# Two feed-forward pairs, a lambda and a last passage: three small reorderings in a two-layer streaming encoder step

## The chip, the cores and the metric

The kernel runs on one core of a Trainium2 chip. The metric is the device time of one execution in microseconds (us), lower is better. Five engines work side by side: TensorE (PE in the rows; PEld is its weight load), VectorE (DVE), ScalarE (ACT), GpSimd (POOL) and SyncE (SP), each with an in-order queue. They meet through semaphores only.

## The reference

Two layers run on 512 prompt frames and 32 sample frames, which lie side by side as 544 columns. Layer 0 mixes with gated linear attention, layer 1 with differential attention (two softmaxes of each head, subtracted with a learned lambda). Each mixer is followed by a gated feed-forward with a causal convolution of width 3:

```python
h = modulate(rms_norm(x, norm_mix[i]), sh1, sc1)
if i % N_MIXERS == 0:
    mix, S_fin = gla_mixer(h, S0, ...)
else:
    q, k, v = diff_project(h, diff_w_in[j], diff_q_norm[j], diff_k_norm[j])
    lam = jnp.exp(jnp.sum(lq1 * lk1)) - jnp.exp(jnp.sum(lq2 * lk2)) + lam_init
    o = diff_attend(q, k, v, 0, lam)          # softmax 0 - lam * softmax 1
    o = rms_norm(o, diff_norm[j]) * (1.0 - lam_init)
    mix = einsum('bthe,hed->btd', o, diff_w_out)
x = x + gt1[:, None, :] * mix
h = modulate(rms_norm(x, norm_ffn[i]), sh2, sc2)
f, cst_new = conv_ffn(h, cst, ffn_w_in[i], ffn_conv_w[i], ffn_conv_b[i], ffn_w_out[i])
x = x + gt2[:, None, :] * f
```

All data are float32. Projections are made as three matmuls of split operands (high with high, low with high, high with low part).

## The kernel before

**Blocks and units.** All projections form one stream of weight blocks of 256 columns (`BL`), each with an own load by SyncE into `w_raw` (three buffers), a `split` on ScalarE (the high part, into `w_hi` or `w_third`) and a `low` on VectorE (the low part, into `w_lo`). TensorE waits for `low` of a block before the block's first unit. A block has four units: two column tiles `t` of 128 by two halves of the 544 columns (272 each). A unit is 24 matmuls of 128x272 (eight contraction tiles by three) into one of the eight banks of the PSUM. `place_units` gives each unit its bank; `U_PREV` is the unit that had the bank before, and `bank_free` makes TensorE wait until it is evacuated.

**Pairs.** The first two blocks after each norm are run as a pair of eight units, in `first_pair`: all first halves (units 0 to 3), then all second halves (units 4 to 7), since the norm finishes the columns half by half. Units 0, 1, 4, 5 belong to the pair's first block, 2, 3, 6, 7 to its second. Units 0, 1 and 4, 5 follow the norm's tiles as these are made. `PAIR_BANKS` gives their banks. In between stands `stats`: the sums of squares of half 0 and 1 go to banks 4 and 5, where ScalarE's `half_root` reads them.

**The norm at such a place.** For each half and each of eight tiles: VectorE scales (`half_scaled`, `sq`), ScalarE adds the shift (`half_modulated`, `h_hi`), VectorE makes the rest (`h_lo`). `half_tiles(which, half, ks)` issues this on VectorE. A norm needs the squares of all eight tiles of `xT` (ScalarE's `square`), which GpSimd adds up in `acc`, before TensorE can sum them over partitions.

**The feed-forward** (`ffn`). The up blocks alternate between the u and gate halves. For each tile ScalarE copies the unit of the first half into `up` (`head_in`), then the second half's pieces, and makes the first convolution term; VectorE adds the other two. For gate tiles ScalarE also makes the SiLU and casts the product (`act_hi`), each of which waits for VectorE. After the norm ScalarE first makes the SiLU of `c_row`. The evacuation order of the pair is units 0, 1, 4, 5, then 2, 6, 3, 7. The third up block, `("up", l, 0, 2)`, had banks 4, 5, 7, 6 of its own, all later up blocks have banks 0 to 3 in turn.

**The lambda.** Ahead of layer 1's attention VectorE makes the two sums of the lambda (`lam_ok`), ScalarE the exponentials (`lam_exp`), VectorE the rest (`lam_done`). ScalarE waits for this and then evacuates the pair of the first keys and queries, `("dk", 0)` and `("dq", 0)`, squares first and then the scaled values into `kT` and `qT`.

**The last passage.** The output projection of the attention ends with `doutB`: 16 units in four banks in turn, eight for half 0 and eight for half 1, which VectorE adds to `xT` (`last_out`). The norm of half 0 begins while the units of half 1 are still being added; the order of both on VectorE and of squares, shifts and the two half splits on ScalarE is written out by hand.

Of the kernel before, what the change touches and what calls it, by code (L numbers as in the profile page):

```python
# [10 lines left out]
ALU = mybir.AluOpType  # L11
# [9 lines left out]
KT = D // P  # L21
TP, TS = 512, 32
T = TP + TS
# [17 lines left out]
SCALE = HD ** -0.5  # L41
LAM_INIT = 0.8 - 0.6 * math.exp(-0.3)
# [51 lines left out]
BL = stream_blocks()  # L94
BN = {name: n for n, name in enumerate(BL)}
# [9 lines left out]
PAIRS = [(("gout", 2), ("gout", 3)), (("down", 0, 3, 2), ("down", 0, 3, 3)), (("dk", 0), ("dq", 0))]  # L105
PAIRS += [(("up", l, 0, 0), ("up", l, 0, 1)) for l in range(DEPTH)]
PAIR_OF = {a: b for a, b in PAIRS}
PAIRED = [x for pair in PAIRS for x in pair]
PAIR_BANKS = [0, 1, 2, 3, 7, 6, 0, 1]
block_kt = lambda n: CH[BL[n][2]] if BL[n][0] == "down" else KA if BL[n][0] == "doutA" else KT  # L110

UNITS = []
# [10 lines left out]
FIRST_U, LAST_U = [min(us) for us in BU], [max(us) for us in BU]  # L123
# [6 lines left out]
def place_units():  # L130
    bank, prev = [], []
    last, counts, small = {}, {True: 0, False: 0}, 0
    for u, (n, t, half) in enumerate(UNITS):
        kind = BL[n][0]
        if BL[n] in PAIRED:
            at = u - FIRST_U[BN[next(a for a, z in PAIRS if BL[n] in (a, z))]]
            b = at % 4 if kind in ("gout", "down") else PAIR_BANKS[at]
        elif kind == "up" and BL[n][2:] == (0, 2):
            b = (4, 5, 7, 6)[u - FIRST_U[n]]
        elif BL[n] in KMAJOR:  # L140
            b = u - FIRST_U[n]
        elif kind in ("qk", "v", "r", "dq", "dk", "dv", "doutA"):
            b = small % 2
            small += 1
        else:
            b = (u - FIRST_U[n]) % 4
        bank.append(b)
        prev.append(last.get(b))
        last[b] = u
    evac_no = [0] * len(UNITS)  # L150
    for n, name in enumerate(BL):
        if name[0] == "up" and name in PAIRED:
            us = BU[n] if name not in PAIR_OF else [BU[n][i] for i in (0, 2, 1, 3)]
        elif name in PAIR_OF:
            us = range(FIRST_U[n], FIRST_U[n] + 8)
        elif name in PAIRED:
            us = []
        else:
            us = range(FIRST_U[n], LAST_U[n] + 1)
        for u in us:  # L160
            on_act = BL[UNITS[u][0]][0] in ACT_KINDS
            counts[on_act] += 1
            evac_no[u] = counts[on_act]
    return bank, prev, evac_no
# [44 lines left out]
H_BASE = (0, KT, 2 * KT, 4 * KT, 6 * KT)  # L209
# [17 lines left out]
block_units = lambda name: BU[BN[name]]  # L227
pair_units = lambda name: list(range(FIRST_U[BN[name]], FIRST_U[BN[name]] + 8))
# [61 lines left out]
def hybrid_stream_step(nc, A, O):  # L290
    ctx = ExitStack()
    with ctx:
# [3 lines left out]
        def sem(name):  # L296
            return ctx.enter_context(nc.semaphore(name))
# [4 lines left out]
        h_hi = sb("h_hi", [P, KT, T], F32R)  # L302
        h_lo = sb("h_lo", [P, KT, T], F32R)
# [61 lines left out]
        up = sb("up", [P, 2, W + 2], c=f)  # L365
# [9 lines left out]
        st = sb("st", [P, 96], c=d)  # L375
# [91 lines left out]
        up_ok, conv_ok, silu_ok, prod_ok, act_hi_ok, act_ok = (sem(x) for x in (  # L467
            "up_ok", "conv_ok", "silu_ok", "prod_ok", "act_hi_ok", "act_ok"))

        lam_ok, lam_exp, lam_done = sem("lam_ok"), sem("lam_exp"), sem("lam_done")  # L470
        hsum_ok, hlog_ok, hinv_ok, heads_ok = (sem(x) for x in ("hsum_ok", "hlog_ok", "hinv_ok", "heads_ok"))
        sc_ok, mx_ok, p_ok, a_ok, a_turned, a_out, av_ok, av_out = (sem(x) for x in (
            "sc_ok", "mx_ok", "p_ok", "a_ok", "a_turned", "a_out", "av_ok", "av_out"))
# [686 lines left out]
        def _(act):  # L1160
# [48 lines left out]
            def half_modulated(which, half, ks):  # L1209
                l, sub = which // 2, which % 2  # L1210
                for k in ks:
                    act.wait_ge(xs_ok, XS_BASE[which] + KT * half + k + 1)
                    for grp, c in ((0, slice(0, HALF)),) if half == 0 else ((0, slice(HALF, TP)), (1, slice(TP, T))):
                        ins = A_(h_hi[:, k, c], sq[:, k % 2, c], ACT.Identity, bias=ada[:, l, 3 * sub * KT + k, grp:grp + 1])
                    ins.then_inc(h_hi_ok, 1)
# [48 lines left out]
            def evacuate_all(us):  # L1264
                for u in us:
                    evacuate(u)
# [301 lines left out]
            def heads_turned(p, part_, bank):  # L1568
# [4 lines left out]
                else:  # L1573
                    A_(hi[:, k:k + 2, TP:T], ps[:, bank, 0:2 * TS].rearrange("p (j t) -> p j t", j=2), ACT.Identity,
                       scale=st[:, 1:2]).then_inc(od_hi_ok, 1)

            act.wait_ge(lam_ok, 1)
            A_(st[:, 4:6], st[:, 2:4], ACT.Exp).then_inc(lam_exp, 1)
            act.wait_ge(lam_done, 1)
            us, dv0 = pair_units(("dk", 0)), block_units(("dv", 0))  # L1580
            evacuate_all(us[0:7])
            head_norms(0, 0)
            evacuate(us[7])
            head_norms(0, 1)
# [46 lines left out]
            half_modulated(3, 0, (1,))  # L1631
            square(3, 4, 1)
            square(3, 5, 1)
            half_modulated(3, 0, (2,))
            square(3, 6, 1)
            square(3, 7, 1)
            half_modulated(3, 0, (3,))
            split(BN[("up", 1, 0, 1)], 0)
            half_modulated(3, 0, (4, 5))
            split(BN[("up", 1, 0, 1)], 1)  # L1640
# [7 lines left out]
        def _(dve):  # L1648
# [86 lines left out]
            def half_tiles(which, half, ks):  # L1735
                l, sub = which // 2, which % 2
                for k in ks:
                    if k == 0:
                        dve.wait_ge(rstd_ok, sums_at(which, half))
                        half_scaled(which, half, 0)  # L1740
                    if k + 1 < KT:
                        half_scaled(which, half, k + 1)
                    dve.wait_ge(h_hi_ok, NORM_H[which] + KT * half + k + 1)
                    for grp, c in ((0, slice(0, HALF)),) if half == 0 else ((0, slice(HALF, TP)), (1, slice(TP, T))):
                        ins = STT(out=h_lo[:, k, c], in0=sq[:, k % 2, c], scalar=ada[:, l, 3 * sub * KT + k, grp:grp + 1], in1=f32(h_hi[:, k, c]),  # L1745
                                  op0=ALU.add, op1=ALU.subtract)
                    ins.then_inc(h_ok, 1)
# [61 lines left out]
            def evacuate_all(us):  # L1809
                for u in us:  # L1810
                    evacuate(u)
# [263 lines left out]
            dve.wait_ge(nc_stored, 16)  # L2075
            dve.wait_ge(lam_loaded, 16)
            dve.wait_ge(h_ok, H_BASE[4])
            TT(h_smp2[:, :, :], f32(h_hi[:, :, TP:T]), f32(h_lo[:, :, TP:T]), ALU.add).then_inc(smp_ok, 1)
            lp = lam_in[:, :, :].rearrange("p (a b) d -> p a b d", b=2)
            step.then(TT(lp[:, :, 0, :], lp[:, :, 0, :], lp[:, :, 1, :], ALU.mult))  # L2080
            dve.tensor_reduce(st[:, 2:4], lp[:, :, 0, :], AX_X, ALU.add).then_inc(lam_ok, 1)
            dve.tensor_scalar(st[:, 0:1], q_gain, SCALE, None, ALU.mult)
            dve.tensor_scalar(st[:, 1:2], d_gain, 1.0 - LAM_INIT, None, ALU.mult)
            dve.wait_ge(lam_exp, 1)
            step.then(TT(st[:, 6:7], st[:, 5:6], st[:, 4:5], ALU.subtract))
            step.then(dve.tensor_scalar(st[:, 7:8], st[:, 6:7], -LAM_INIT, None, ALU.add))
            STT(out=st[:, 8:9], in0=cpart("isc1"), scalar=st[:, 7:8], in1=cpart("isc0"), op0=ALU.mult, op1=ALU.add).then_inc(lam_done, 1)

            def heads_normalised(p, idx):
                if p >= NPAIR:  # L2090
# [140 lines left out]
            last_out(DOUT_B[KT:KT + 4])  # L2231
            half_tiles(3, 0, (0,))
            last_out(DOUT_B[KT + 4:KT + 6])
            half_tiles(3, 0, (1,))
            last_out(DOUT_B[KT + 6:])
            half_tiles(3, 0, range(2, KT))
            low(BN[("up", 1, 0, 1)])
            half_tiles(3, 1, range(KT))
            ffn(1)
# [121 lines left out]
```

## Time and profile before

| what | us |
|---|---|
| median of 3 runs | 1397.14 (1396.92 to 1397.16) |
| span of the profiled execution | 1395.4 |
| runs' median less this span | 1.74 |
| TensorE busy | 1374.3 |
| VectorE busy | 950.7 |
| ScalarE busy | 655.0 |
| GpSimd busy | 89.5 |

The span runs from the first to the last instruction of one profiled execution; the runs' time holds what lies around it as well. The TensorE clock was granted in full all the way (1.000). An idle time of an engine other than TensorE costs nothing unless TensorE ends up waiting for it.

### The profile page before, as it was taken

What the parts mean: (1) busy time and instruction counts of PE and PEld (TensorE: products, weight loads), DVE (VectorE), ACT (ScalarE), POOL (GpSimd) and SP (SyncE); (2) the same over time, 40 slices, a digit from 0 to 9 for tenths busy, and PEclk for the clock granted to TensorE, in tenths of its full rate; (3) what the DMA queues carried; (4) which work ended last, traced back from release to release, by engine and by line L of the source; (5) the groups of instructions that cost most, each with busy time, mean ns of one, the idle gap of its engine ahead of it and who ended that gap; (6) DMA issues with size and microseconds to landing.
All of it is one profiled execution on the core that took longest, in us unless ns stands there. A gap on an engine that the chain in (4) does not pass through costs nothing.

```text
span 1395.4 us, 26322 instructions
## 1 busy us (share of the span) xinstructions
PE 1374.3 (98%) x10882; PEld 1294.7 (93%) x10882; DVE 950.7 (68%) x1595; ACT 655.0 (47%) x1458; POOL 89.5 (6%) x149
## 2 busy tenths in 40 slices
PE   8999999999999999999999999999899999999999
PEld 6878888999999999999888888889899999999999
DVE  5688677479988788678765646576798654554554
ACT  5543434366553353351565555653665542552430
POOL 0000000210000000000300000000300000000000
PEclk9999999999999999999999999999999999999999
DMA  9644542244445444534523224112244222223222
GB/s 378 238 167 147 178 152 84 72 171 135 161 144 171 171 157 133 193 115 148 182 107 106 103 98 137 63 62 93 96 161 135 77 78 91 91 69 114 76 71 103
DMA packets 38014, 182.42 MB, mean 131 GB/s; under 512 B 4294, under 2 KB 6854, under 8 KB 26632
## 3 DMA queue, kind: packets, MB, share of 16 engines
q1 hardware_dynamic: 22984, 126.98, 26.4%
q0 software_dynamic: 14912, 53.78, 11.1%
q8 instruction: 86, 1.41, 0.4%
q14 instruction: 32, 0.26, 0.1%
HBM read 172.82 MB, written 7.91 MB: 130 GB/s over the span
## 4 chain that ended last, share of the span: by engine, by line
PE 91%; DVE 4%; ACT 3%; issue 1%; DMA 0%; POOL 0%; SPq 0%; DVEq 0%; POOLq 0%; ACTq 0%
PE ps L656 27%; PE ps L658 26%; PE ps L657 26%; PE ps L1065 2%; PE ps L1115 1%; DVE sq L1732 1%; DVE h_lo L1745 1%; PE ps L1024 1%; PE ps L1087 1%; PE ps L913 1%; PE ps L909 1%; ACT w_hi L1173 1%; PE ps L694 1%; PE ps L900 1%; PE ps L746 1%
## 5 line engine op out<-in xcount | busy, mean ns | idle before, releaser
L658 PE MATMUL ps<-h_hi,w_lo 128*128 128x272 f32 x2048 | 592.5, 289 | 0.0
L656 PE MATMUL ps<-h_hi,w_hi 128*128 128x272 f32 x1952 | 569.1, 292 | 5.5 <-ACT up L1452 1.7
L657 PE MATMUL ps<-h_lo,w_hi 128*128 128x272 f32 x1952 | 561.3, 288 | 0.0
L658 PEld LDWEIGHTS ps<-h_hi,w_lo 128*128 128x128 f32 x2048 | 385.0, 188 | 0.0
L656 PEld LDWEIGHTS ps<-h_hi,w_hi 128*128 128x128 f32 x1952 | 367.4, 188 | 15.8 <-issue 6.7
L657 PEld LDWEIGHTS ps<-h_lo,w_hi 128*128 128x128 f32 x1952 | 367.9, 188 | 1.0 <-issue 1.0
L1173 ACT CAST w_hi<-w_raw 128x2048 fp32r<-128x2048 f32 (+2 forms) x106 | 179.3, 1692 | 196.6 <-PE ps L658 169.1
L1660 DVE TENSOR_TENSOR w_lo<-w_raw,w_hi 128x2048 fp32r<-128x2048 f32 (+2 forms) x105 | 215.2, 2049 | 66.9 <-ACT w_hi L1173 66.2
L657 PE MATMUL ps<-act_lo,w_hi 128*128 128x272 f32 (+1 forms) x704 | 203.8, 290 | 0.0
L656 PE MATMUL ps<-act_hi,w_hi 128*128 128x272 f32 (+1 forms) x704 | 203.5, 289 | 0.0
L658 PE MATMUL ps<-act_hi,w_lo 128*128 128x272 f32 (+1 forms) x704 | 203.2, 289 | 0.0
L1821 DVE SCALAR_TENSOR_TENSOR xT<-ps,ada,xT 128x272 f32<-128x272 f32 (+2 forms) x264 | 96.9, 402 | 95.6 <-PE ps L658 95.0
L2056 DVE SCALAR_TENSOR_TENSOR cv<-up,vec,cv 128x546 f32<-128x546 f32 x88 | 69.3, 788 | 124.6 <-ACT cv L1491 124.6
L1692 DVE SCALAR_TENSOR_TENSOR a_prod<-a_raw,c_row 128x1025 f32<-128x1025 f32 x112 | 136.9, 1222 | 1.4 <-DMA a_raw<-in_ada_r 1.1
L658 PEld LDWEIGHTS ps<-act_hi,w_lo 128*128 128x128 f32 x704 | 133.2, 189 | 0.0
L656 PEld LDWEIGHTS ps<-act_hi,w_hi 128*128 128x128 f32 x704 | 132.9, 189 | 0.0
L657 PEld LDWEIGHTS ps<-act_lo,w_hi 128*128 128x128 f32 x704 | 132.9, 189 | 0.0
L1485 ACT COPY up<-ps 128x240 f32<-128x240 f32 x88 | 31.9, 362 | 106.2 <-PE ps L658 106.2
L656 PE MATMUL ps<-w_hi,h_hi 128*128 128x256 f32 x256 | 74.3, 290 | 1.8 <-ACT qk L1245 1.4
L1491 ACT ACTIVATE cv<-up,vec 128x546 f32<-128x546 f32 x88 | 74.6, 847 | 2.9
L657 PE MATMUL ps<-w_lo,h_hi 128*128 128x256 f32 x256 | 72.3, 282 | 0.0
L658 PE MATMUL ps<-w_hi,h_lo 128*128 128x256 f32 x256 | 71.9, 281 | 0.0
(285 smaller groups left out, 1766.9 us busy)
## 6 DMA issues: line engine op xcount, KB each, us to landing
w_raw<-in_wst SPq DMA_DIRECT2D x72, 1024.0 KB, 5.0
a_raw<-in_ada_r POOLq DMA_DIRECT2D x56, 512.5 KB, 4.6
w_raw<-in_wst SPq DMA_DIRECT2D x28, 768.0 KB, 4.3
a_raw<-in_ada_g POOLq DMA_DIRECT2D x24, 512.0 KB, 3.6
a_pro<-in_ada_p SPq DMA_DIRECT2D x8, 1024.0 KB, 16.5
v_raw<-in_wst SPq DMA_DIRECT2D x8, 1024.0 KB, 8.2
w_raw<-in_wst SPq DMA_DIRECT2D x10, 512.0 KB, 4.0
xT<-in_xT SPq DMA_DIRECT2D x4, 544.0 KB, 5.3
```

Source lines behind the costliest of these rows:

```text
L656: mm(out, lhs_hi, rhs_hi, start=first, stop=False)
L657: mm(out, lhs_hi, rhs_lo, start=False, stop=False)
L658: return mm(out, lhs_lo, rhs_hi, start=False, stop=last)
L694: ins = mm(ps[TS * j:TS * (j + 1), U_BANK[u], 0:BC], x[:, k, :], v_raw[:, k * BC:(k + 1) * BC], start=(k < 4), stop=(k >= 4), skip_group_c ...
L1065: ins = mm(ps[:, b + c, 0:nk], qT[e, s, j, r * P:(r + 1) * P], kT[e, s, j, 0:nk], start=True, stop=True)
L1173: ins = act.copy(hi_cols(n, c0, c1), low_cols(w_raw, n, c0, c1))
L1485: act.copy(x[:, 2 + HALF:2 + TP], b1[:, 0:PB])
L1491: A_(cv1[:, t, :], x[:, 0:W], ACT.Identity, scale=conv_c[:, 6 * l, ft:ft + 1], bias=conv_c[:, 6 * l + 3, ft:ft + 1]).then_inc(up_ok, 1)
L1660: ins = TT(low_cols(w_lo, n, c0, c1), low_cols(w_raw, n, c0, c1), f32(hi_cols(n, c0, c1)), ALU.subtract)
L1692: STT(out=prod_gla if gla else a_prod[:, :], in0=x, scalar=1.0, in1=c, op0=ALU.mult, op1=ALU.mult, accum_out=ada[:, l, 2 * b + t, grp:grp ...
L1821: ins = STT(out=xT[:, m, c0:c1], in0=src[:, at:at + c1 - c0], scalar=ada[:, l, (gate_row % 6) * KT + m, grp:grp + 1], in1=xT[:, m, c0:c1], ...
L2056: step.then(STT(out=cv1[:, t, :], in0=x[:, 1:W + 1], scalar=w(1), in1=cv1[:, t, :], op0=ALU.mult, op1=ALU.add))
```

## The change

The bank table is split by kind: the pair of the attention keeps its banks, while the last two units of the feed-forward pairs go to banks 4 and 5 (those of the norm sums), and the third up block falls back to banks 0 to 3. On ScalarE, the first two key units are evacuated before the exponentials of lambda, and the wait for `lam_done` is dropped, with the semaphore; instead ScalarE waits for the stored convolution state and for the last tile of the norm. VectorE's small instructions at this place are reordered. In the last passage, the two last outputs (units 14 and 15 of `doutB`) are added to `xT` after tile 3 of the norm instead of after tile 1, and ScalarE shifts tile 3 ahead of the squares 6 and 7.

```diff
-PAIR_BANKS = [0, 1, 2, 3, 7, 6, 0, 1]
+PAIR_BANKS = {"dk": [0, 1, 2, 3, 7, 6, 0, 1], "up": [0, 1, 2, 3, 7, 6, 4, 5]}
...
         if BL[n] in PAIRED:
-            at = u - FIRST_U[BN[next(a for a, z in PAIRS if BL[n] in (a, z))]]
-            b = at % 4 if kind in ("gout", "down") else PAIR_BANKS[at]
-        elif kind == "up" and BL[n][2:] == (0, 2):
-            b = (4, 5, 7, 6)[u - FIRST_U[n]]
+            lead = next(a for a, z in PAIRS if BL[n] in (a, z))
+            at = u - FIRST_U[BN[lead]]
+            b = PAIR_BANKS[lead[0]][at] if lead[0] in PAIR_BANKS else at % 4
...
+            us, dv0 = pair_units(("dk", 0)), block_units(("dv", 0))
+            act.wait_ge(nc_stored, 16)
+            act.wait_ge(h_ok, H_BASE[4])
+            evacuate_all(us[0:2])
             act.wait_ge(lam_ok, 1)
             A_(st[:, 4:6], st[:, 2:4], ACT.Exp).then_inc(lam_exp, 1)
-            act.wait_ge(lam_done, 1)
-            us, dv0 = pair_units(("dk", 0)), block_units(("dv", 0))
-            evacuate_all(us[0:7])
+            evacuate_all(us[2:7])
...
             half_modulated(3, 0, (1,))
             square(3, 4, 1)
             square(3, 5, 1)
-            half_modulated(3, 0, (2,))
+            half_modulated(3, 0, (2, 3))
             square(3, 6, 1)
             square(3, 7, 1)
-            half_modulated(3, 0, (3,))
             split(BN[("up", 1, 0, 1)], 0)
             half_modulated(3, 0, (4, 5))
             split(BN[("up", 1, 0, 1)], 1)
...
             dve.wait_ge(h_ok, H_BASE[4])
-            TT(h_smp2[:, :, :], f32(h_hi[:, :, TP:T]), f32(h_lo[:, :, TP:T]), ALU.add).then_inc(smp_ok, 1)
             lp = lam_in[:, :, :].rearrange("p (a b) d -> p a b d", b=2)
+            dve.tensor_scalar(st[:, 0:1], q_gain, SCALE, None, ALU.mult)
+            dve.tensor_scalar(st[:, 1:2], d_gain, 1.0 - LAM_INIT, None, ALU.mult)
             step.then(TT(lp[:, :, 0, :], lp[:, :, 0, :], lp[:, :, 1, :], ALU.mult))
             dve.tensor_reduce(st[:, 2:4], lp[:, :, 0, :], AX_X, ALU.add).then_inc(lam_ok, 1)
-            dve.tensor_scalar(st[:, 0:1], q_gain, SCALE, None, ALU.mult)
-            dve.tensor_scalar(st[:, 1:2], d_gain, 1.0 - LAM_INIT, None, ALU.mult)
+            TT(h_smp2[:, :, :], f32(h_hi[:, :, TP:T]), f32(h_lo[:, :, TP:T]), ALU.add).then_inc(smp_ok, 1)
             dve.wait_ge(lam_exp, 1)
...
             last_out(DOUT_B[KT:KT + 4])
             half_tiles(3, 0, (0,))
             last_out(DOUT_B[KT + 4:KT + 6])
-            half_tiles(3, 0, (1,))
+            half_tiles(3, 0, (1, 2, 3))
             last_out(DOUT_B[KT + 6:])
-            half_tiles(3, 0, range(2, KT))
+            half_tiles(3, 0, range(4, KT))
             low(BN[("up", 1, 0, 1)])
             half_tiles(3, 1, range(KT))
```

## Rows read from the trace of the kernel before

**Rows 1.** The page, busy time, share and instructions of each engine.

```profile
PE 1374.3 (98%) x10882; PEld 1294.7 (93%) x10882; DVE 950.7 (68%) x1595; ACT 655.0 (47%) x1458; POOL 89.5 (6%) x149
```

**Rows 2.** TensorE's waits over the whole span: total us, times, longest.

```profile
PE ps L656 <- DVE h_lo L1745: 3.4, 6, 1.4
...
PE ps L656 <- ACT up L1452: 1.7, 2, 0.9
```

**Rows 3.** Timeline of TensorE, pair of layer 0: start, duration, idle before.

```profile
303.26 0.29 PE L658 MATMUL ps<-h_hi,w_lo 128*128 128x272 f32 x1
304.28 0.40 PE L656 MATMUL ps<-h_hi,w_hi 128*128 128x272 f32 x1 [0.73 <-ACT up L1452]
304.52 0.29 PE L657 MATMUL ps<-h_lo,w_hi 128*128 128x272 f32 x1
...
310.39 0.29 PE L656 MATMUL ps<-h_hi,w_hi 128*128 128x272 f32 x1
...
322.47 0.29 PE L656 MATMUL ps<-h_hi,w_hi 128*128 128x272 f32 x1
```

**Rows 4.** Timeline of ScalarE, the same stretch.

```profile
303.86 0.65 ACT L1452 COPY up<-ps 128x272 f32<-128x272 f32 x2
...
322.01 0.65 ACT L1501 CAST act_hi<-cv 128x546 fp32r<-128x546 f32 x1 [2.44 <-DVE cv L2065]
322.56 0.38 ACT L1452 COPY up<-ps 128x272 f32<-128x272 f32 x1
```

**Rows 5.** Timeline of VectorE, the same stretch.

```profile
307.73 2.29 DVE L1660 TENSOR_TENSOR w_lo<-w_raw,w_hi 128x2048 fp32r<-128x2048 f32 x1 [0.19 <-ACT w_hi L1173]
```

**Rows 6.** Timeline of TensorE at the lambda, pair of the first keys.

```profile
709.73 0.29 PE L658 MATMUL ps<-h_hi,w_lo 128*128 128x272 f32 x1
710.73 0.39 PE L656 MATMUL ps<-h_hi,w_hi 128*128 128x272 f32 x1 [0.71 <-ACT kT L1260]
```

**Rows 7.** Timeline of ScalarE at the lambda.

```profile
709.90 0.40 ACT L1259 ACTIVATE sq<-ps 128x272 f32<-128x272 f32 x1 [0.67 <-DVE st L2087]
710.19 0.48 ACT L1260 ACTIVATE kT<-ps,vec 128x272 f32<-128x272 f32 x1
```

**Rows 8.** Timeline of VectorE at the lambda: the norm's last tile.

```profile
707.27 0.63 DVE L1745 SCALAR_TENSOR_TENSOR h_lo<-sq,ada,h_hi 128x240 fp32r<-128x240 f32 x2 [0.23 <-ACT h_hi L1214]
```

**Rows 9.** Timeline of TensorE, last passage.

```profile
990.75 0.39 PE L656 MATMUL ps<-h_hi,w_hi 128*128 128x272 f32 x1 [1.37 <-DVE h_lo L1745]
...
994.69 0.39 PE L656 MATMUL ps<-h_hi,w_hi 128*128 128x272 f32 x1
...
997.43 0.39 PE L656 MATMUL ps<-h_hi,w_hi 128*128 128x272 f32 x1
```

**Rows 10.** Timeline of VectorE, last passage.

```profile
987.28 1.01 DVE L1745 SCALAR_TENSOR_TENSOR h_lo<-sq,ada,h_hi 128x272 fp32r<-128x272 f32 x1
988.22 1.15 DVE L1821 SCALAR_TENSOR_TENSOR xT<-ps,ada,xT 128x240 f32<-128x240 f32 x4
...
995.09 2.28 DVE L1660 TENSOR_TENSOR w_lo<-w_raw,w_hi 128x2048 fp32r<-128x2048 f32 x1
```

**Rows 11.** Timeline of ScalarE, last passage.

```profile
989.81 0.52 ACT L1214 ACTIVATE h_hi<-sq,ada 128x272 fp32r<-128x272 f32 x1
990.24 1.03 ACT L1173 CAST w_hi<-w_raw 128x1024 fp32r<-128x1024 f32 x1
```

**Rows 12.** Timeline of GpSimd, last passage.

```profile
988.14 0.78 POOL L590 TENSOR_TENSOR acc<-acc,sq 128x272 f32<-128x272 f32 x1
```

**Rows 13.** Timeline of GpSimd, the norm ahead of layer 0's feed-forward.

```profile
279.55 0.91 POOL L590 TENSOR_TENSOR acc<-acc,sq 128x272 f32<-128x272 f32 x1 [3.65 <-ACT sq L1187]
```

**Rows 14.** Timeline of VectorE at the same time.

```profile
279.87 0.89 DVE L1732 SCALAR_TENSOR_TENSOR sq<-xT,gain,acc 128x272 f32<-128x272 f32 x1
```

**Rows 15.** Timeline of TensorE, layer 1's fourth up block.

```profile
1028.88 0.29 PE L656 MATMUL ps<-h_hi,w_hi 128*128 128x272 f32 x1
```

**Rows 16.** Timeline of ScalarE, the same place.

```profile
1028.97 0.38 ACT L1452 COPY up<-ps 128x272 f32<-128x272 f32 x1
```

More of the change, by code:

```diff
@@ L468, in hybrid_stream_step @@
             "up_ok", "conv_ok", "silu_ok", "prod_ok", "act_hi_ok", "act_ok"))
-        lam_ok, lam_exp, lam_done = sem("lam_ok"), sem("lam_exp"), sem("lam_done")
+        lam_ok, lam_exp = sem("lam_ok"), sem("lam_exp")
         hsum_ok, hlog_ok, hinv_ok, heads_ok = (sem(x) for x in ("hsum_ok", "hlog_ok", "hinv_ok", "heads_ok"))
@@ L2086, in _ @@
             step.then(dve.tensor_scalar(st[:, 7:8], st[:, 6:7], -LAM_INIT, None, ALU.add))
-            STT(out=st[:, 8:9], in0=cpart("isc1"), scalar=st[:, 7:8], in1=cpart("isc0"), op0=ALU.mult, op1=ALU.add).then_inc(lam_done, 1)
+            STT(out=st[:, 8:9], in0=cpart("isc1"), scalar=st[:, 7:8], in1=cpart("isc0"), op0=ALU.mult, op1=ALU.add)
             def heads_normalised(p, idx):
```

## The prediction

> **What bounds the kernel now.** I read the page first: TensorE is busy for 98% of the span [rows 1], and the chain that ended last runs through its matmuls, so a change can only win where TensorE stands still, and loses wherever it makes TensorE stand still anew. Next I read who TensorE waited for over the whole span: the waits are few and short, and the three kinds that the change touches are there, the ScalarE copy into `up` twice and `h_lo` six times [rows 2], and a wait for `kT` at the lambda. Then I read the three stages in order of time, engine by engine, looking at each TensorE gap for what ended it, and at what each engine had queued behind it.
>
> One wait costs more than the time the row names. Steady matmuls start 0.125 us apart (47 of them from 304.52 to 310.39). At 304.28 the gap is 1.02, and the next start comes 0.24 later instead of 0.125, so the stop costs 0.895 + 0.115 = 1.01 us [rows 3]. I call the 0.115 the restart.
>
> **Part A: banks of the feed-forward pair (both layers).** No work is added. Units 6 and 7 of the pair wrote banks 0 and 1, which hold units 0 and 1 until ScalarE has copied unit 0 out. ScalarE reaches this copy at 303.86 and TensorE starts 0.42 later [rows 3, 4]. In the banks of the norm sums nothing is in the way, so units 6 and 7 start at 303.385 and are done, 48 matmuls later, at 309.40.
>
> What is late next? First the weights of the third up block. Its low part is made on VectorE from 307.73 for 2.29, to 310.02 [rows 5], behind ScalarE's own late start, which no bank changes. TensorE starts 0.06 after such an end (997.43 after 995.09 + 2.28) [rows 9, 10]. So the third block starts at 310.08, with the restart 310.195, against 310.39 before: of 1.01 us only 0.20 is left.
>
> Second, the third block now lies in banks 0 to 3 instead of 4, 5, 7, 6, and the fourth block still in 0 to 3. Before, the fourth block's first unit needed only the copy of unit 6. Now it needs the copy of the third block's own first unit. ScalarE makes that copy at 322.56, right behind the cast of `act_hi` at 322.01 [rows 4], which waits for VectorE's product. This chain of ScalarE and VectorE starts at the end of the norm and never waits for TensorE up to here, so it does not move. TensorE can start at 322.56 + 0.42 = 322.98, with the restart 323.095. Before it started at 322.47 [rows 3]. So layer 0 ends 0.62 us later, not earlier. After that ScalarE has caught up, and TensorE has no wait in the feed-forward to hide this in. In layer 1 the same two events stand 706.41 later, at 1028.97 and 1028.88 [rows 15, 16], so the same 0.62 holds there. Bounds of the term for a layer: -1.01 if neither new wait bites, -0.20 if only the weights do, +0.62 with both, as the instruction order says. I take +0.62.
>
> **Part B: keys ahead of lambda.** ScalarE now starts on the keys when the last `h_lo` is done, at 707.27 + 0.63 = 707.90 [rows 8], instead of at 709.90 after the lambda. The evacuation of unit 0 takes until 710.19 + 0.48, that is 0.77 [rows 7], so its bank is free at 708.7. TensorE would arrive at 709.73 + 0.125 = 709.855, and waits no more; before, it started at 710.73 [rows 6]. That returns 0.875 + 0.115 = 0.99 us. Behind it, the exponential of lambda costs ScalarE a little after unit 1, and units 2 to 5 follow some 1.7 us earlier than before, so the head sums, behind unit 6, find their squares ready. VectorE has the lambda steps and `h_smp2` in another order but as many, and nothing waits for them in this stretch. The DMA loads of the next weights hang on TensorE's units, not on this order. Bounds: 0 if a later wait takes it all, -0.99 if none does. I take -0.99.
>
> **Part C: two outputs of the last passage later.** VectorE's instructions are the same and as many; the order changes on VectorE and ScalarE. TensorE's wait of 1.37 for tile 2 [rows 9] goes, because the tile's `h_lo` comes ahead of the two outputs. Then:
>
> Tile 1's `h_lo` ends at 987.28 + 1.01 = 988.29 [rows 10]. The scaling of tile 3 comes next, at 988.32. GpSimd is adding squares from 988.14 to 988.92 [rows 12], and where a scaling began under such an addition it took 0.89 [rows 13, 14] instead of 0.5. In rows like these it ends 0.30 after the addition, here at 989.22. The outputs that ran in this place before read PSUM and were not stretched: 1.15 for four [rows 10]. `h_lo` of tile 2 (989.13), the scaling of tile 4 (989.66) and `h_lo` of tile 3 (990.08) follow: an instruction of 0.5 overlaps the next by 0.07 to 0.09 where only the engine holds it (988.22 against 988.29 [rows 10]), and starts some 0.03 after the end where it needs the result. The two outputs start at 990.50 instead of 988.22.
>
> The Trainium skill, "SBUF — State Buffer", section "SBUF: two separate sides", says that a VectorE instruction with two SBUF inputs and a GpSimd instruction that reads SBUF exclude each other for the whole instruction. By it the scaling would run 0.5 after the addition's end, to 989.42, and the sum would come out 0.2 later. The rows of this case give 0.30, so the rule's direction holds and its size is a little too large.
>
> What hangs on those outputs? ScalarE's squares 6 and 7, and, in its queue behind them, the first half of the next weight split, and behind that the shifted tile 4. The split began at 990.24, 2.02 after the outputs, with one tile of 0.43 between that now comes earlier [rows 10, 11]. So now it begins at 990.50 + 2.02 - 0.43 = 992.09. It takes 1.03, so tile 4 is shifted from 993.11 to 993.64, and VectorE, with nothing else to do, stands still for it and makes `h_lo` 4 at 993.68. The remaining tiles run behind ScalarE's second half split and VectorE's own two instructions a tile: `h_lo` 5 at 994.63, 6 at 995.58 to 996.08, 7 at 996.26. The low weights of the pair's second block start at 996.68 instead of 995.09 [rows 10]. TensorE's step of tile 6, and with it the sums of the second half, comes at 996.14 instead of 994.69 [rows 9], and the second half's whole chain (root, tiles, the copies into `up`) is 1.45 later. TensorE's stop moves from tile 2 to tile 4 and grows to some 2.7 us. Its second block starts 1.59 later than 997.43 [rows 9].
>
> With part A, TensorE meets this chain again at the fourth block's copy: 1028.97 + 1.45 + 0.42 + 0.115 = 1030.955 against 1028.88 [rows 15, 16]. Parts A and C together give layer 1 +2.07. Bounds of C: -1.37 if the tile's wait simply goes, 0 if the second half's chain doesn't move, +1.04 if the scaling isn't stretched, +1.45 as worked out. I take +1.45, since each step is an order in a queue.
>
> **The sum.** +0.62 - 0.99 + 2.07 = +1.70 us. The profiled execution spans 1395.4; the median of the runs is 1397.14, so 1.74 lies around the span and is not touched. Forecast: 1397.1 for the span, 1398.8 for the time. What a measurement of this kernel can tell from no change is about 0.2%, 2.8 us, so this is "same", on the slow side.
>
> **The rivals.**
> 1. The second half's chain in the last passage doesn't move: the delay is covered before the sums. Against it: VectorE has no idle time there, and tile 4 stands behind the split. Then 0.62 + 0.62 - 0.99 = +0.25, 1397.4.
> 2. The lambda's gain is lost, because another wait (the head sums or the first value rows) takes its place. Against it: ScalarE's evacuations there get 1.7 us of room. Then +0.62 + 2.07 = +2.69, 1399.8.
> 3. More collisions of GpSimd and VectorE in the last passage, now that the additions fall between other instructions: one or two more stretches of 0.5 us each. Then 1399.3 to 1399.8.
> 4. The other side: the chain of ScalarE and VectorE isn't what limits, TensorE is, and all four stops go: 2 x 1.01 + 0.99 + 1.37 = 4.4 us, 1392.8. It decides from the point where the third block's low weights come before 309.40 and its first copy ends before 322.3. Against it: 310.02 and 322.94 in the trace, on a chain that doesn't see the banks.
>
> **How the numbers follow.** My sum with its small terms, 1398.2 to 1399.2: 0.63. Rival 1: 0.16. Rival 2: 0.05. Rival 3: 0.09. Rival 4: 0.05. The last 0.02 is for anything slower still. Faster by over 0.2% is below 1394.3, rival 4 alone: 0.05. Slower by over 0.2% is above 1399.9: half of rivals 2 and 3 and the rest, 0.09 with rounding. Within: 0.86. The range from 1397.0 to 1399.8 leaves out rival 4, the upper half of rivals 2 and 3 and the rest.
>
> **What would show it.** Right: in layer 0 no TensorE gap at the pair's unit 6, a short one (about 0.6) for `w_lo` at 310, and a new one of about 0.7 for a copy into `up` near 323, with ScalarE's rows at the same times as before. At the lambda, no wait for `kT` and the following rows 1 us closer. In the last passage, a TensorE wait of over 2 us for `h_lo` two tiles later than before, and the copy into `up` near 1010 shifted 1.4 later against the stage's start. Wrong: if ScalarE's chain in layer 0 itself starts earlier, if the new gap near 323 is missing, or if VectorE's low weights of the second block don't move.

## The result, and the profile after

The changed kernel takes 1400.1 us (median of 17 runs, 1398.84 to 1405.45), the kernel before 1397.16 us beside it (17 runs). The ratio is 1.0023 [1.0017, 1.0029]: slower by 2.9 us, where the prediction had 1.70.

The page of the changed kernel, its first lines, answers to [rows 1]:

```profile
span 1398.3 us, 26323 instructions
## 1 busy us (share of the span) xinstructions
PE 1375.5 (98%) x10882; PEld 1295.9 (93%) x10882; DVE 950.1 (68%) x1595; ACT 654.1 (47%) x1458; POOL 89.2 (6%) x149
```

The instructions are as many as before, and TensorE is busy 1.2 us longer. The span grew by 2.9 us, so the loss lies inside it, and the same matmuls took a little longer as well.

**Layer 0.** The TensorE timeline of the changed kernel around the pair and the up blocks, answering to [rows 3] (start, duration, the instruction, and in brackets the idle time ahead of it and who ended it):

```profile
303.38 0.29 PE L655 MATMUL ps<-h_hi,w_hi 128*128 128x272 f32 x1
...
310.10 0.39 PE L655 MATMUL ps<-h_hi,w_hi 128*128 128x272 f32 x1 [0.55 <-DVE w_lo L1660]
...
323.10 0.36 PE L655 MATMUL ps<-h_hi,w_hi 128*128 128x272 f32 x1 [0.66 <-ACT up L1451]
```

Unit 6 of the pair starts at 303.38 without a gap. The two new waits stand where they were put: for the low weights of the third block at 310.10 (forecast 310.195) and for that block's own first copy at 323.10 (forecast 323.095). ScalarE's timeline answers to [rows 4]:

```profile
303.89 0.65 ACT L1451 COPY up<-ps 128x272 f32<-128x272 f32 x2
...
322.57 0.38 ACT L1451 COPY up<-ps 128x272 f32<-128x272 f32 x1
```

Both copies are within 0.03 of before: ScalarE's chain indeed does not see the banks.

**The lambda.** ScalarE's timeline answers to [rows 7]:

```profile
708.40 0.40 ACT L1258 ACTIVATE sq<-ps 128x272 f32<-128x272 f32 x1 [0.75 <-issue]
708.69 0.48 ACT L1259 ACTIVATE kT<-ps,vec 128x272 f32<-128x272 f32 x1
```

The key's first evacuation ends at 709.17 instead of 710.67, and TensorE has no wait for `kT` any more. Ahead of this stage the changed kernel is 0.42 late. TensorE's first matmul behind the head sums, before the change and after it:

```profile
714.29 0.69 PE L656 MATMUL ps<-h_hi,w_hi 128*128 128x272 f32 x1
713.72 0.69 PE L655 MATMUL ps<-h_hi,w_hi 128*128 128x272 f32 x1
```

So the changed kernel is now 0.57 early. That is a gain of 0.99, as forecast.

**The last passage.** It starts 0.61 early (tile 1's `h_lo` at 986.67 against 987.28 [rows 10]). VectorE's timeline:

```profile
986.67 1.01 DVE L1745 SCALAR_TENSOR_TENSOR h_lo<-sq,ada,h_hi 128x272 fp32r<-128x272 f32 x1
987.72 0.88 DVE L1732 SCALAR_TENSOR_TENSOR sq<-xT,gain,acc 128x272 f32<-128x272 f32 x1
...
989.88 1.15 DVE L1821 SCALAR_TENSOR_TENSOR xT<-ps,ada,xT 128x240 f32<-128x240 f32 x4
990.95 0.49 DVE L1732 SCALAR_TENSOR_TENSOR sq<-xT,gain,acc 128x272 f32<-128x272 f32 x1
992.89 0.50 DVE L1745 SCALAR_TENSOR_TENSOR h_lo<-sq,ada,h_hi 128x272 fp32r<-128x272 f32 x1 [1.45 <-ACT h_hi L1213]
...
995.89 2.28 DVE L1660 TENSOR_TENSOR w_lo<-w_raw,w_hi 128x2048 fp32r<-128x2048 f32 x1
```

The stretched scaling is there (0.88), the outputs start at 989.88, and VectorE stands still for 1.45 until ScalarE has shifted tile 4. Put back by the 0.61, the outputs start at 990.49 (forecast 990.50), `h_lo` of tile 4 at 993.50 (993.68), and the low weights of the second block at 996.50 (996.68). ScalarE's timeline of the same stretch, answering to [rows 11]:

```profile
990.53 0.96 ACT L1186 ACTIVATE sq<-xT 128x272 f32<-128x272 f32 x2 [1.37 <-DVE xT L1821]
991.40 1.03 ACT L1172 CAST w_hi<-w_raw 128x1024 fp32r<-128x1024 f32 x1
992.34 0.93 ACT L1213 ACTIVATE h_hi<-sq,ada 128x272 fp32r<-128x272 f32 x2
...
998.83 0.49 ACT L1205 ACTIVATE acc<-ps,eps 128x272 f32<-128x272 f32 x1 [3.39 <-PE ps L769]
```

The reader sees ScalarE wait 1.37 for the late outputs, then do the squares and the half split, and only then shift tiles 4 and 5. The last line is the first step of the second half's root, which needs TensorE's sums. In the kernel before it was:

```profile
996.66 0.49 ACT L1206 ACTIVATE acc<-ps,eps 128x272 f32<-128x272 f32 x1 [2.02 <-PE ps L770]
```

Counted from tile 1's `h_lo` the root is 12.16 us away instead of 9.38: 2.78 later, where the prediction had 1.45. So something between the outputs and this root took 1.33 us more than the forecast of the queues. TensorE's timeline shows what:

```profile
989.07 0.39 PE L655 MATMUL ps<-h_hi,w_hi 128*128 128x272 f32 x1 [0.31 <-DVE h_lo L1745]
...
993.45 0.39 PE L655 MATMUL ps<-h_hi,w_hi 128*128 128x272 f32 x1 [2.40 <-DVE h_lo L1745]
...
995.34 0.60 PE L655 MATMUL ps<-h_hi,w_hi 128*128 128x272 f32 x1
...
995.96 0.43 PE L657 MATMUL ps<-h_hi,w_lo 128*128 128x272 f32 x1
996.19 0.43 PE L655 MATMUL ps<-h_hi,w_hi 128*128 128x272 f32 x1
...
1031.64 0.36 PE L655 MATMUL ps<-h_hi,w_hi 128*128 128x272 f32 x1 [0.65 <-ACT up L1451]
```

The stop has moved from tile 2 to tile 4 and its wait is 2.40; the prediction looked for over 2. Tile 6 starts at 995.34, 8.67 after tile 1's `h_lo`, against 7.41 before (994.69 [rows 9]): 1.26 later, a little less than forecast. From tile 6 to the root it takes 3.49 instead of 1.97, and these 1.52 are what the prediction did not have. There two matmuls start 0.23 apart (995.96, 996.19), where steady ones start 0.125 apart. The windows of the same stretch (window in us, its length, busy time and count of each engine, the granted clock, DMA share, GB/s) name the reason:

```profile
core 0: us, PE busy (x) PEld busy (x) DVE busy (x) ACT busy (x) POOL busy (x), PEclk, DMA share, GB/s
992.00:994.00 2.00, 0.55 (x4) 0.56 (x5) 1.08 (x3) 2.00 (x4) 0.06 (x1) 1.00 0.00 0
994.00:996.00 2.00, 2.00 (x13) 1.71 (x12) 1.79 (x5) 1.15 (x3) 0.00 (x0) 0.79 0.00 0
996.00:998.00 2.00, 2.00 (x8) 1.77 (x8) 2.00 (x1) 0.00 (x0) 0.00 (x0) 0.50 0.00 0
998.00:1000.00 2.00, 2.00 (x13) 1.82 (x13) 0.36 (x2) 0.92 (x2) 0.91 (x3) 0.86 0.04 8
1000.00:1002.00 2.00, 2.00 (x18) 2.00 (x17) 1.73 (x7) 1.31 (x4) 0.96 (x2) 1.00 0.72 207
```

TensorE resumed at 993.45 at the full 2.4 GHz, and somewhere in the next window the granted clock fell to 1.2 GHz (0.50 all through 996 to 998); by 1000 it was back. The columns to read together are PE busy and PEclk: TensorE is busy 2.00 of 2.00 us, with 8 matmuls instead of 18. What ran at the low clock is the end of tile 5, tile 6 and the sums of the second half, which the root waits for, and the start of tile 7 behind them.

The other runs say that a loss of clock is the common case: the mean clock of the span was 1.000 in 3 of the 17 runs of the changed kernel (1398.84, 1398.90 and 1399.05) and below it (0.997 to 0.999) in 14, whose median is 1400.28. The three are at the forecast of 1398.8. Where in the span a run lost its clock is known for the profiled one alone.

### The profile page after: what moved, and what is told of

Its sections match the earlier page's. It is cut to its first block, busy times and chain, and to the rows that moved or that the text cites. A ratio compares the mean times of both kernels' runs of the same rounds, so it can differ in the third digit from the quotient of the medians.

```text
span 1398.3 us, 26323 instructions
## 1 busy us (share of the span) xinstructions
PE 1375.5 (98%) x10882; PEld 1295.9 (93%) x10882; DVE 950.1 (68%) x1595; ACT 654.1 (47%) x1458; POOL 89.2 (6%) x149
## 4 chain that ended last, share of the span: by engine, by line
PE 89%; DVE 4%; ACT 3%; issue 2%; DMA 0%; POOL 0%; SPq 0%; DVEq 0%; POOLq 0%; ACTq 0%
PE ps L655 26%; PE ps L657 25%; PE ps L656 25%; PE ps L1064 2%; PE ps L1114 1%; ACT w_hi L1172 1%; PE ps L1023 1%; DVE w_lo L1660 1%; DVE sq L1732 1%; DVE h_lo L1745 1%; PE ps L1086 1%; PE ps L912 1%; PE ps L908 1%; PE ps L693 1%; PE ps L899 1%
```

## The experiments

The theory going in: the queue steps of the prediction hold, and the excess of about 1.3 us is the clock's fall behind the longer stop. The rivals: the parts cost more than forecast by their queues, or they collide with each other. The first four runs shared one chip, where the kernel before took 1397.44 (median of 33 runs).

**Part A alone.** Only the banks: the table of the diff, and the third up block in banks 0 to 3.

```diff
-PAIR_BANKS = [0, 1, 2, 3, 7, 6, 0, 1]
+PAIR_BANKS = {"dk": [0, 1, 2, 3, 7, 6, 0, 1], "up": [0, 1, 2, 3, 7, 6, 4, 5]}
...
-        elif kind == "up" and BL[n][2:] == (0, 2):
-            b = (4, 5, 7, 6)[u - FIRST_U[n]]
```

> Part A alone on the kernel before (units 6 and 7 of the feed-forward pairs in banks 4 and 5, third up block in banks 0 to 3). My theory: both new waits bite in both layers, a short one for the low weights at the third block and one for the copy into up at the fourth, +0.62 us a layer, some 0.2 of layer 0's given back at the next norm: +1.0 to +1.25 us, about 1398.3, clock 1.000. Rival (the banks only free TensorE): -0.4 to -2.0 us, 1396.8 or less. Rival (part A is neutral and all the loss is the last passage): 1397.2.

Measured: 1398.72 (11 runs, 1398.16 to 1399.59), ratio 1.0007 [0.9999, 1.0016], so +1.28. All 11 runs had a mean clock of 1.000. TensorE's timeline of this kernel:

```profile
309.98 0.39 PE L655 MATMUL ps<-h_hi,w_hi 128*128 128x272 f32 x1 [0.57 <-DVE w_lo L1659]
...
322.97 0.36 PE L655 MATMUL ps<-h_hi,w_hi 128*128 128x272 f32 x1 [0.66 <-ACT up L1451]
...
1029.70 0.36 PE L655 MATMUL ps<-h_hi,w_hi 128*128 128x272 f32 x1 [0.66 <-ACT up L1451]
```

Both new waits come without the other parts, in both layers. The interval of the time alone reaches to no change; the rows decide.

**Part B alone.** Only the lambda's two edits: the first two evacuations ahead of the exponentials, the wait for `lam_done` gone, VectorE's small steps reordered.

```diff
...
+            evacuate_all(us[0:2])
             act.wait_ge(lam_ok, 1)
             A_(st[:, 4:6], st[:, 2:4], ACT.Exp).then_inc(lam_exp, 1)
-            act.wait_ge(lam_done, 1)
...
-            evacuate_all(us[0:7])
+            evacuate_all(us[2:7])
```

> Part B alone (first two key units evacuated ahead of the lambda). My theory: the wait for kT goes and nothing takes its place: -0.99 us, 1396.2, clock 1.000. Rival (another wait takes it): 1397.2.

Measured: 1396.57 (11 runs), ratio 0.9993 [0.9985, 1.0002], so -0.87, with a span of 1394.5 against 1395.4. By the times alone this is no difference; it is of the size and sign that the rows of the changed kernel give for the lambda, and this kernel's own trace has no wait for `kT` either.

**Part C alone.** Only the order of the last passage, on both engines.

```diff
-            half_modulated(3, 0, (2,))
+            half_modulated(3, 0, (2, 3))
...
-            half_modulated(3, 0, (3,))
...
-            half_tiles(3, 0, (1,))
+            half_tiles(3, 0, (1, 2, 3))
...
-            half_tiles(3, 0, range(2, KT))
+            half_tiles(3, 0, range(4, KT))
```

> Part C alone (two last outputs after tile 3, ScalarE's order with it). Theory of the queues: +1.45 us from the chain of the second half, 1398.6, with a wait of TensorE of about 2.4 for tile 4. Theory of the clock on top of it: after this wait the granted clock falls to 0.5 for some 2 to 3 us in most runs, +1.3 more: median about 1399.9, runs spread over several us, and only the runs at clock 1.000 near 1398.6. Rival (the clock fall needs parts A or B too): all runs at clock 1.000 and 1398.6.

Measured: 1399.84 (11 runs, 1398.42 to 1401.32), ratio 1.0012 [1.0003, 1.0021], so +2.40 alone. Four runs had a mean clock of 1.000 (median 1398.54), seven less (median 1400.04). The windows of its profile:

```profile
994.00:996.00 2.00, 1.83 (x8) 1.83 (x9) 1.93 (x5) 1.71 (x3) 0.00 (x0) 0.55 0.00 0
996.00:998.00 2.00, 2.00 (x12) 2.00 (x12) 1.82 (x3) 0.16 (x1) 0.00 (x0) 0.60 0.00 0
```

The fall belongs to part C and needs neither other part: here too TensorE had a wait of 2.40 for `h_lo` of tile 4, ended at 994.17, and the clock is at 0.55 in the window behind it.

**The changed kernel, with TensorE kept busy in the stop.** Eight matmuls of 128 columns, whose result nothing reads, ahead of the wait for tile 4.

```diff
                     for k in range(KT):
+                        if which == 3 and half == 0 and k == 4:
+                            keep_warm(8, 6)
                         pe.wait_ge(h_ok, H_BASE[stage] + KT * half + k + 1)
```

> The changed kernel with 8 matmuls of 128 columns added into an idle bank just ahead of TensorE's long wait for tile 4 in the last passage; their result is used by nothing. Theory of the clock: TensorE stays busy over the wait, the granted clock stays at 1.000, and all runs come to 1398.8 to 1399.1, where the changed kernel's fastest runs are: 1.0 to 1.3 us less than its median of 1400.1. Rival (the excess over the forecast is the order of the queues, not the clock): 1400.1 or more, as the added matmuls give nothing back.

Measured: 1399.01 (11 runs), ratio 1.0012 [1.0003, 1.0021], so +1.57; ten runs had a mean clock of 1.000, with a median of 1399.0, and one was 1403.52 at 0.999. TensorE's timeline and, below it, the windows behind the stop:

```profile
991.18 1.95 PE L762 MATMUL ps<-cst 128*128 128x128 f32 x16
993.75 0.39 PE L655 MATMUL ps<-h_hi,w_hi 128*128 128x272 f32 x1 [0.62 <-DVE h_lo L1747]
...
995.64 0.39 PE L655 MATMUL ps<-h_hi,w_hi 128*128 128x272 f32 x1
```

```profile
994.00:996.00 2.00, 2.00 (x15) 1.70 (x14) 1.79 (x5) 1.45 (x3) 0.00 (x0) 1.00 0.00 0
996.00:998.00 2.00, 2.00 (x15) 1.84 (x14) 2.00 (x2) 0.39 (x1) 0.12 (x1) 1.00 0.00 0
```

The unused matmuls, 16 rows in the trace, fill 1.95 of the stop; the wait for tile 4 ends no sooner, since VectorE and ScalarE are as before. All that changes is the clock behind it, 1.00 in place of 0.79 and 0.50. The second half's root, on ScalarE:

```profile
997.61 0.49 ACT L1207 ACTIVATE acc<-ps,eps 128x272 f32<-128x272 f32 x1 [1.88 <-PE ps L769]
```

That is 10.65 after tile 1's `h_lo` (986.96): 1.27 more than before, where the prediction had 1.45. The intervals of the two ratios overlap, so it is the rows that tell the theories apart. Tile 6 starts 8.68 after tile 1's `h_lo` (8.67 in the changed kernel's profile), so no queue got shorter. From there to the root it takes 1.97, as before the change, and not 3.49. The times agree: ten of these 11 runs took 1399.27 or less, and 14 of the changed kernel's 17 took 1399.90 or more. The rival of longer queues falls, and that of colliding parts too, since all three parts are in.

**The order on ScalarE.** The next four runs shared another chip, where the kernel before took 1397.43 (32 runs). First part C with VectorE's order as changed, but ScalarE's first half split and tile 4 ahead of the squares that wait for the late outputs.

```diff
-            half_modulated(3, 0, (2,))
+            half_modulated(3, 0, (2, 3))
+            split(BN[("up", 1, 0, 1)], 0)
+            half_modulated(3, 0, (4,))
             square(3, 6, 1)
             square(3, 7, 1)
-            half_modulated(3, 0, (3,))
-            split(BN[("up", 1, 0, 1)], 0)
-            half_modulated(3, 0, (4, 5))
+            half_modulated(3, 0, (5,))
```

> Part C alone, but with ScalarE's first half split and the shift of tile 4 ahead of the squares 6 and 7. My theory (the loss of part C is ScalarE's queue: tile 4 behind squares that wait for the late outputs, and the split): VectorE no longer stands still, TensorE's wait for tile 4 shrinks from 2.4 to about 1, the clock stays at 1.000 in all runs, and the second half is at most 0.4 us later than in the kernel before (one scaling stretched under a GpSimd addition): 1397.2 to 1397.8. Rival (the late outputs themselves are the loss, through the sums): as part C alone, 1398.6 at clock 1.000 and more where it falls.

Measured: 1397.57 (11 runs, 1397.11 to 1397.99), ratio 0.9998 [0.9989, 1.0007]. All runs had a mean clock of 1.000. TensorE's timeline:

```profile
989.63 0.39 PE L656 MATMUL ps<-h_hi,w_hi 128*128 128x272 f32 x1 [0.31 <-DVE h_lo L1745]
...
992.97 0.39 PE L656 MATMUL ps<-h_hi,w_hi 128*128 128x272 f32 x1 [1.37 <-DVE h_lo L1745]
```

The wait of 1.37 is as long as the one of [rows 9], and stands at tile 4 instead of tile 2. So what made part C cost time is that on ScalarE tile 4, with the half split ahead of it, stood behind squares that waited for the late outputs. VectorE's new order by itself wins nothing here: the stop has only another place.

**Part A with other banks for the third and fourth block.** The third block takes 0, 1, 7, 6 and the fourth 2 to 5, so that the fourth does not need the third's own banks.

```diff
+UP_BANKS = {(0, 2): (0, 1, 7, 6), (0, 3): (2, 3, 4, 5)}
...
+        elif kind == "up" and BL[n][2:] in UP_BANKS:
+            b = UP_BANKS[BL[n][2:]][u - FIRST_U[n]]
```

> Part A with other banks behind it: third up block in 0, 1, 7, 6 and fourth in 2, 3, 4, 5, so that the fourth block waits for no unit of the third. My theory: the wait near 323 for the copy into up goes, that for the low weights near 310 stays; 0.2 us less than the kernel before in each layer, 1396.9 to 1397.2, and 1.2 to 1.6 less than part A as it was made. Rival (the third block's own banks are not the cause): as part A, about 1398.5.

Measured: 1397.13 (11 runs), ratio 0.9997 [0.9989, 1.0006], so -0.30, and 1.58 below part A as made when each is set against its own kernel before. The waits of TensorE in layer 0 (285 to 325) list the low weights alone (waits for, total, times, longest):

```profile
PE ps L658 <- DVE w_lo L1662: 0.8, 2, 0.6
```

The copy's wait is gone, and what is left is near the bound of -0.20 a layer that the prediction gave for the case that only the weights' wait comes.

**ScalarE's start ahead of the pair.** Both new waits of part A hang on ScalarE starting late, behind the table load and SiLU of `c_row`. This kernel leaves the banks and the last passage as before, has part B, and puts the table load right behind the second half's root and the SiLU, in four pieces, between the last tiles' shifts, where ScalarE waits for VectorE.

```diff
-                half_modulated(which, 1, range(KT))
+                if which == 1:
+                    last_tiles(which)
+                else:
+                    half_modulated(which, 1, range(KT))
+
+            def last_tiles(which):
+                act.preload_act_table_set("silu_and_others")
+                half_modulated(which, 1, range(4))
+                act.wait_ge(crow_in, 48 + 16 * (which // 2))
+                for q in range(4):
+                    half_modulated(which, 1, (4 + q,))
+                    c = slice(q % 2 * D // 2, (q % 2 + 1) * D // 2)
+                    ins = A_(c_row[:, q // 2, c], c_row[:, q // 2, c], ACT.Silu)
+                ins.then_inc(crow_ok, 1)
...
-                act.wait_ge(crow_in, 48 + 16 * l)
-                A_(c_row[:, :, 0:D], c_row[:, :, 0:D], ACT.Silu).then_inc(crow_ok, 1)
...
-            half_modulated(3, 1, range(KT))
+            last_tiles(3)
```

> The kernel before with part B, and ScalarE's table load and SiLU of c_row taken out of the start of the feed-forward: the table is loaded behind the second half's root, the SiLU made in four pieces between the last tiles of the norm. No bank is changed. My theory (ScalarE's late start is what TensorE waits for): unit 0 is copied by 302.5, TensorE's stop at unit 6 goes in both layers without any change of banks, -1.01 each, and -0.99 from part B: about 1394.3, clock 1.000. Rival (the pieces delay the tiles by as much as they save): -0.99 alone or little more, 1396.2.

Measured: 1394.17 (10 runs, 1393.74 to 1399.96), ratio 0.9981 [0.9972, 0.9991], so -3.26, and faster than both kernels. ScalarE's timeline in layer 0:

```profile
291.05 1.28 ACT L1451 ACT_TABLE_LOAD   x1
...
297.51 0.62 ACT L1457 ACTIVATE c_row<-c_row 128x512 f32<-128x512 f32 x1
...
301.08 0.62 ACT L1457 ACTIVATE c_row<-c_row 128x512 f32<-128x512 f32 x1
302.00 0.68 ACT L1465 COPY up<-ps 128x272 f32<-128x272 f32 x2 [0.30 <-DVE up L2050]
302.98 0.36 ACT L1496 COPY up<-ps 128x240 f32<-128x240 f32 x1 [0.30 <-PE ps L658]
```

The copy of unit 0 starts at 302.00 instead of 303.86 [rows 4], ahead of TensorE's arrival at unit 6, so the stop of 1.01 goes in both layers without any change of banks; TensorE's waits between 285 and 325 are 0.2 in all, for the low weights. At 302.98 ScalarE waits for TensorE: the start is as early as it can be of use.

**The same with part A's banks.**

```diff
-PAIR_BANKS = [0, 1, 2, 3, 7, 6, 0, 1]
+PAIR_BANKS = {"dk": [0, 1, 2, 3, 7, 6, 0, 1], "up": [0, 1, 2, 3, 7, 6, 4, 5]}
...
-        elif kind == "up" and BL[n][2:] == (0, 2):
-            b = (4, 5, 7, 6)[u - FIRST_U[n]]
```

> As the run with the early SiLU and part B, and part A as it was made on top. My theory: with ScalarE's chain some 3 us earlier neither the third block's low weights nor the third block's first copy are late, so part A costs nothing: the same time as without it within 0.2 us, about 1394.3, no wait near 310 and 323. Rival (part A costs 0.62 a layer by itself): 1395.5.

Measured: 1395.04 (11 runs), ratio 0.9981 [0.9972, 0.9989], 0.87 above the run before. The expectation that the banks cost nothing here was a miss. TensorE's timeline:

```profile
322.00 0.36 PE L655 MATMUL ps<-h_hi,w_hi 128*128 128x272 f32 x1 [0.24 <-ACT up L1464]
```

The fourth block still waits for the third's own first copy, 0.24 in layer 0 and, at 1026.79, 0.24 in layer 1. Against the changed kernel, ScalarE's copy of unit 0 comes 1.54 earlier here (302.35 against 303.89), but the copy of the third block's first unit only 1.10 earlier (321.47 against 322.57). So part A's second cost comes from its banks, and with this early start of ScalarE it gets smaller but stays.

**Unused matmuls in the stop that was always there.** Two runs on a third chip, where the kernel before took 1397.48 (18 runs), put four such matmuls ahead of tile 2's wait of 1.37: the kernel with the early SiLU, and the kernel before.

```diff
+                        if which == 3 and half == 0 and k == 2:
+                            keep_warm(4, 6)
```

> The early SiLU with part B, and 4 unused matmuls of 128 columns ahead of TensorE's wait of 1.37 for tile 2 in the last passage. Theory of the clock (any long stop of TensorE in this passage can be followed by a fall, the longer the oftener): all runs at clock 1.000 and within 0.2 us of the fastest without them, 1393.7 to 1394.0 where the median without them was 1394.2. Rival (the falls of that run have another cause): runs below 1.000 as before, same median.

> The kernel before with the same 4 unused matmuls at the same place and nothing else. Theory of the clock: the few runs of the kernel before that lie 0.4 to 1 us above its fastest, at clock 0.999, go; median 1397.0 to 1397.3, no gain beyond that, since the wait itself stays. Rival: no difference in their number.

Measured: 1394.25 (8 runs), ratio 0.9978 [0.9968, 0.9988], and 1397.62 (11 runs), ratio 1.0001 [0.9991, 1.001]. Neither gains on the same kernel without them, though both were expected to, by some tenths. Runs with a mean clock below 1.000 were 1 of 8 against 4 of 10 without, and 2 of 11 against 17 of 83: too few to tell. These runs are inconclusive, and they bound the worth: where most runs keep the clock in any case, the median has little to gain from it.

## Why the prediction was right or wrong, point by point

**Part A: right.** Both waits came at the forecast places, within 0.1 us, and ScalarE's copies did not move. The term of +0.62 a layer measured +0.63 at 323.10 against 322.47 [rows 3], and +0.70 from the next matmul on: the start came 0.53 after the copy's instead of 0.42, and the restart, which the forecast had counted in the start, came on top. The step "TensorE has no wait in the feed-forward to hide this in" held; but of layer 0's 0.70 a part of 0.28 was given back later, in the norm ahead of the attention (the changed kernel is 0.70 late at 682 and 0.42 late at 696), a cover that the prediction had not looked for. The run of part A alone, +1.28, is at the term for both layers.

**Part B: right.** The term of -0.99 measured -0.99.

**Part C: the queues right, the price of the stop wrong.** The collision with GpSimd was forecast as 0.89 and took 0.88; the scaling ends at 988.60. The addition it met ended at 988.30 (986.35 + 1.95 for the two of them), 0.30 earlier, which is the size that the rows gave. By the Trainium skill's rule ("SBUF — State Buffer", section "SBUF: two separate sides") it would have ended an estimated 0.5 after the addition, its own unhindered length; here too the measurement differs from it. The move of the stop to tile 4, its 2.40 of wait, VectorE's halt and the late low weights all stand within 0.2. The second half's chain, counted from tile 1's `h_lo`, was forecast 1.45 later; with TensorE kept busy it was 1.27 later, and in the changed kernel's profile 2.78.

The step that failed is the term "+1.45 as worked out" for that chain, at the sentence that TensorE's stop "moves from tile 2 to tile 4 and grows to some 2.7 us". The stop was priced as waiting time, and all its followers at the full clock. What the runs showed in its place is a second price: in the profile the granted clock fell behind this stop, on matmuls that the root waits for, which cost 1.52 us from tile 6 to the root, and 14 of 17 runs had a mean clock below 1.000. The excess over the forecast is smaller, 1.33 at the root and 1.30 at the fourth block's start (1031.64 + 0.61 - 1028.88 [rows 15] = 3.37 late, forecast 2.07), since the chain itself was forecast 0.18 too long (1.45 against 1.27). The three windows miss (0.21 + 0.50 + 0.14) x 2.00 = 1.70 us of full clock. The Trainium skill, "TensorE: Matmul & The Clock Gate", section "Terms", puts the penalty of a throttled stretch at about its time times the missing share of the clock, which is this same sum; in the trace 1.52 arrived at the root, a little less than the formula gives. Why the rest did not arrive is not shown.

**The sum.** It is read by setting each of TensorE's matmuls against the same one of the kernel before. In the changed kernel's profile they are 0.70 late behind layer 0's fourth block, 0.42 late behind the next norm, 0.57 early behind the lambda, 0.61 early at the last passage, and 2.82 late from layer 1's fourth block to the end; the span grew by 2.9. The last step, 3.43, is 2.78 for C's chain up to the root and 0.65 for part A. With TensorE kept busy the same places give 0.70 and 0.68 late, 0.29 and 0.32 early, and 1.61 late at the end, where the time says +1.57. Its last step is 1.93: 1.27 for the chain and 0.66 for part A. The two last steps differ by 1.50, which is the price of the clock. The forecast was +1.70. That the runs at full clock meet it is in part luck: part A was forecast some 0.1 too small in the two layers together, the chain 0.18 too long.

**The rivals.** Rival 1 fell: the second half's chain moved. Rival 2 fell: the lambda's gain stayed. Rival 3 named nearly the right size (1399.3 to 1399.8) for the wrong reason: the trace has the one stretched scaling that was forecast. Rival 4 fell, but run by run its weak point showed: the stops at unit 6 do go if ScalarE's chain starts earlier, which the early SiLU did and the banks could not. The clock was no rival at all, although the wait in question grew from 1.37 to 2.40 us, and the page of the profile has a row for it.

**What stays open.** The same kernel, with the same stop, keeps its clock in some runs and loses it in others. The kernel before, whose longest wait in this stretch is 1.37, had a mean clock below 1.000 in 17 of 83 runs, part B alone in 4 of 11 and part A alone in none of 11; no run here tells what decides. Why part A's loss shrinks in the norm ahead of the attention was read off the traces, not tried: ScalarE waits there 0.6 for a weight load in the kernel before, 0.3 in the changed one, which gets 0.28 back, 0.2 with part A alone, which gets 0.35 back, and 0.6 with TensorE kept busy, which gets back 0.02. The early SiLU with the split-first order of the last passage and the spread banks together was not tried.

## What to carry to other kernels

When a stop of an engine goes, look for the next arrival behind it and for who else now uses the freed place: here the bank that was no longer in the way moved the wait to the low weights and then to a copy; other banks took the copy's wait away again, but the time was won only by starting the late engine earlier. When an instruction is moved back, list what its reader's queue holds behind the reader, since a wait at the head of an in-order queue delays every later tile. And a stop of TensorE that grows to some microseconds may cost twice, once as waiting and once as matmuls at 1.2 GHz right behind it; read the granted clock in short windows before calling the excess a longer queue.

## What the runs showed of the hardware

By the windows the clock did not fall during the stop but while TensorE was working again: in the changed kernel's profile TensorE resumed at 993.45, the window from 992 to 994 shows 1.00, and the following two 0.79 and 0.50. With part C alone it fell about when TensorE resumed (994.17): the 0.55 of the window from 994 leaves some 0.2 us of it at the full clock. A reader who looks at the clock of the stop itself sees nothing.

The length of the stop alone does not decide. The profile with the early SiLU and part A's banks has the old wait for tile 2, 1.38 until 989.11, and a fall behind it (columns as above):

```profile
988.00:990.00 2.00, 0.89 (x6) 0.90 (x6) 1.96 (x4) 2.00 (x4) 0.75 (x1) 0.92 0.58 246
990.00:992.00 2.00, 2.00 (x10) 2.00 (x10) 1.89 (x6) 1.57 (x4) 0.00 (x0) 0.50 0.00 0
```

The kernel before has the same wait (1.37) and 1.00 all the way in its profile. With eight unused matmuls in the stop of the changed kernel (1.95 us in the trace), 10 of 11 runs kept the clock, and the wait for tile 4 ended no later for them. A table load on ScalarE took 1.28 us and the next instruction started right behind it (292.35 after 291.05 + 1.28), so that it could be moved to where ScalarE otherwise waits for VectorE.
